# Down weights of the experts loaded with two neighbouring rows in each partition

## The reference

```
# for each expert e; h has 1024 columns, the expert's inner width is 3584
y   = (silu(h @ w_gate[e]) * (h @ w_up[e])) @ w_down[e]
out = out + combine[:, e] * y          # combine: weights of the top 2 of 8
```

## Time and profile before

| | us |
|---|---|
| median of three runs | 1332.88 |
| the three runs | 1332.56 to 1333.57 |
| the profiled execution | 1336.58 |
| its span, first to last instruction | 1335.0 |
| TensorE busy in it | 1305.1 (98%) |
| VectorE busy | 1134.6 (85%) |
| ScalarE busy | 936.9 (70%) |
| GpSimd busy | 149.3 (11%) |
| granted TensorE clock, mean | 0.998 of full speed |

### The profile page before, as it was taken

How to read it: one execution, slowest core, us unless ns; L and a number is a source line. 1 busy time by engine, 2 the same in 40 slices (tenths; PEclk the granted TensorE clock), 3 DMA queues, 4 the chain that set the end, 5 groups by cost and what they waited for, 6 DMA issues and landing times.

```text
span 1335.0 us, 17153 instructions
## 1 busy us (share of the span) xinstructions
PE 1305.1 (98%) x6789; PEld 1074.4 (80%) x6790; DVE 1134.6 (85%) x840; ACT 936.9 (70%) x800; POOL 149.3 (11%) x163
## 2 busy tenths in 40 slices
PE   9999999999999999999999999999999999999997
PEld 8879888898687678878887887788778878887886
DVE  6867666677678899999889999999999998989997
ACT  6675444465876777787777778777877787778774
POOL 3410000011042691000000000000000000000010
PEclk9999999999999999999999999999999999999999
DMA  9846555545369999999999999999999999999994
GB/s 319 247 156 199 190 190 189 189 157 188 121 227 289 395 394 394 395 387 394 363 387 394 393 366 395 395 392 372 394 395 384 358 388 395 392 360 384 396 395 189
DMA packets 199175, 430.81 MB, mean 323 GB/s; under 512 B 9784, under 2 KB 42832, under 8 KB 199088
## 3 DMA queue, kind: packets, MB, share of 16 engines
q1 hardware_dynamic: 193952, 415.40, 86.0%
q0 software_dynamic: 4592, 13.50, 2.7%
q10 hardware_dynamic: 544, 0.75, 0.2%
HBM read 417.56 MB, written 7.36 MB: 318 GB/s over the span
## 4 chain that ended last, share of the span: by engine, by line
PE 83%; DVE 8%; DMA 4%; ACT 2%; issue 2%; POOL 1%; SPq 0%; DVEq 0%; ACTq 0%; POOLq 0%
PE ps L1655 80%; DVE w_low L1156 6%; ACT w_high L808 2%; DMA raw<-in_moe_w_up 2%; PE ps L1982 1%; DMA raw<-in_w_in 1%; POOL work_b L615 1%; PE ps L1681 0%; PE ps L1817 0%; DMA hT_both<-hpad 0%; DMA work_b<-in_conv_w 0%; PE ps L1926 0%; DVE work_a L1530 0%; DVE act_both L1480 0%; DVE work_a L1513 0%
## 5 line engine op out<-in xcount | busy, mean ns | idle before, releaser
L1156 DVE TENSOR_TENSOR w_low<-raw,w_high 128x2048 fp32r<-128x2048 f32 x387 | 891.4, 2309 | 120.0 <-ACT w_high L808 117.9
L808 ACT ACTIVATE w_high<-raw 128x2048 fp32r<-128x2048 f32 x389 | 744.1, 1915 | 251.1 <-PE ps L1655 238.1
L1655 PE MATMUL ps<-w_high,hT_both 128*128 128x512 f32 (+1 forms) x1696 | 529.0, 389 | 3.2 <-DVE w_low L1156 3.1
L1655 PEld LDWEIGHTS ps<-w_high,hT_both 128*128 128x128 f32 x1696 | 316.6, 188 | 69.5 <-issue 3.8
L1655 PE MATMUL ps<-w_low,hT_both 128*128 128x512 f32 (+1 forms) x848 | 327.2, 386 | 0.0
L1655 PE MATMUL ps<-w_high,act_both 128*128 128x512 f32 x960 | 309.1, 393 | 5.7 <-DVE w_low L1156 5.7
L1655 PEld LDWEIGHTS ps<-w_high,act_both 128*128 128x128 f32 x960 | 180.8, 188 | 46.3 <-issue 9.3
L1655 PE MATMUL ps<-w_low,act_both 128*128 128x512 f32 x480 | 187.5, 391 | 0.0
L1655 PEld LDWEIGHTS ps<-w_low,hT_both 128*128 128x128 f32 x848 | 159.6, 188 | 30.4
L1655 PE MATMUL ps<-hT_both,w_high 128*128 128x256 f32 (+1 forms) x640 | 140.4, 339 | 0.0
L1655 PEld LDWEIGHTS ps<-hT_both,w_high 128*128 128x128 f32 x640 | 108.9, 190 | 11.2 <-DVE hT_both L1169 0.4
(11 more groups left out here) (317 smaller groups left out, 809.2 us busy)
## 6 DMA issues: line engine op xcount, KB each, us to landing
raw<-in_moe_w_gate SPq DMA_DIRECT2D x112, 1024.0 KB, 8.8
raw<-in_moe_w_up SPq DMA_DIRECT2D x112, 1024.0 KB, 8.8
raw<-in_moe_w_down SPq DMA_DIRECT2D x112, 1024.0 KB, 8.6
raw<-in_w_in SPq DMA_DIRECT2D x13, 1024.0 KB, 5.3
raw<-in_dense_w_gate SPq DMA_DIRECT2D x11, 1024.0 KB, 5.5
raw<-in_dense_w_up SPq DMA_DIRECT2D x11, 1024.0 KB, 5.5
raw<-in_dense_w_down SPq DMA_DIRECT2D x11, 1024.0 KB, 5.1
raw<-in_w_out SPq DMA_DIRECT2D x8, 1024.0 KB, 7.0
```

What stands on the lines that cost most here:

```text
L808: act.activation(w_part[0][:, s % PART_RING, :], raw[:, s % RAW_RING, :], ACT.Copy).then_inc(w_high_done, 1)
L1156: dve.tensor_tensor(w_part[1][:, q, :], raw[:, r, :], w_part[0][:, q, :], ALU.subtract).then_inc(w_low_done, 1)
L1655: return pe.matmul(out_, lhsT, rhs, start=start, stop=stop, skip_group_check=True)
```

## The change

The view of the experts' down weights now puts rows 2p and 2p + 1 of each 256 in partition p, in one run of 8 KB, in place of rows p and p + 128. Half f of the slot then holds the rows 2p + f. So that each row still meets its own column, the four turns of the product take, for load j and half f, the 128 columns 256 j + f, 256 j + f + 2, and so on: every second column, 8 bytes apart in `prod_t`. Number of loads, bytes, slots, matmuls and transposes stay as they are, and so do the copies after the turn and all of the dense layer.

```diff
         prod_t = work_a[:, 2560:3072]
+        prod_ff = prod_t.rearrange("t (j c f) -> t j c f", j=2, f=2)
...
-        ed_v = moe_w_down.rearrange("o e (k p) n -> (o e) p k n", p=P)
+        ed_v = moe_w_down.rearrange("o e (c p f) n -> (o e) p c (f n)", p=P, f=2)
...
             def down(s, e, g, i, per):
                 for j in range(2):
-                    load(s + j, ed_v[e, :, 4 * g + 2 * j:4 * g + 2 * j + 2, :], 2, i, per)
+                    load(s + j, ed_v[e, :, 2 * g + j:2 * g + j + 1, :], 1, i, per)
...
             def turn_small_act():
                 for f in range(4):
-                    last = pe.transpose(ps[:, 2, f * HALF:(f + 1) * HALF], prod_t[0:HALF, f * P:(f + 1) * P], ident[0:HALF, 0:HALF])
+                    last = pe.transpose(ps[:, 2, f * HALF:(f + 1) * HALF], prod_ff[0:HALF, f // 2, :, f % 2], ident[0:HALF, 0:HALF])
...
             def turn_act():
                 for f in range(4):
-                    last = pe.transpose(ps[:, 2, f * P:(f + 1) * P], prod_t[:, f * P:(f + 1) * P], ident[:, :])
+                    last = pe.transpose(ps[:, 2, f * P:(f + 1) * P], prod_ff[:, f // 2, :, f % 2], ident[:, :])
```

## The result

The changed kernel takes 1335.32 us, the median of 20 runs (1334.09 to 1337.28), against 1333.18 us for the kernel before (20 runs, 1331.35 to 1334.68). The ratio is 1.0017, with a 95% interval from 1.0010 to 1.0023. That is 2.1 us slower. It is under the 0.2% that I called the limit of a measurement, but with 20 runs on each side it stands clear of 1. I had forecast no change.

The account below looks back on a forecast made before the run. TensorE was taken to bound ordinary steps, with loads mattering only at the expert stage's start. Loads -0.3 us, turns 0 and the rest 0 took the median 1332.88 to 1332.6 us, range 1331.0 to 1336.5.

Parts of the forecast that it names:

- no change: Whole kernel: time stays within 1330.7 to 1335.5 us, given chance 0.81.
- What bounds the kernel: Expert stage: TensorE alone sets ordinary steps of 16.81 us; faster loads help only from about 412 to 462 us.
- The loads: Down loads at the expert stage's start: fewer packets save 0.05 us each, 0.3 us for six; bounds -0.5 to +1.2.
- The sign that I named for it: Expert stage start: ScalarE's waits for loads between 400 and 480 us fall from 12.6 us by some tenths.
- The turns: Transposes of the product on TensorE, 49 full and 7 small: strided reading costs 0, upper bound 24.3 us.
- Rival A: Transposes in the 56 turns: strided weight loads cost time, 1336 to 1357 us; chance 0.12.
- the sign that I gave for it: Transposes of the product: weight loads above 150 ns, or a turn above 0.49 us.
- Rival B: Down loads: 8 KB runs, or partitions 8 KB apart in memory, move slower; 1354 us at 3.2 us a load; chance 0.02.
- Rival C: Start of the expert stage: loads bind harder than thought, up to 4.31 us of TensorE idle returns, 1328.6 us; chance 0.05.
- Rival D: Down loads: descriptors are cut at 4 KB anyway, so loads stay unchanged, 1332.9 us; chance 0.15 of the 0.81.
- the sum: Whole kernel: loads -0.3 us, turns 0, the rest 0, giving 1332.6 us against the median.

Follow-up runs that it names:

- the loads alone: The changed kernel with its down loads in 8 KB runs but the transposes reading contiguous columns again: 1333.1 us, ratio 0.9999 to the kernel before.
- turns alone: The kernel before with transposes reading every second column and down loads still in 4 KB runs: 1337.3 us, ratio 1.0027.

## Why the prediction was wrong

**What bounds the kernel** stood. TensorE ends last in the ordinary steps, and the loads matter only at the start of the expert stage; no step there changed its length with the loads alone.

**The loads**: right in kind and within the bounds, a little low in size. I worked out 0.05 us a down load and 0.3 us in all, with a best case of 1.2, from a pair of loads that turned out to be no measure (2.62 us, where a down load takes 2.56). The landings give 0.06 to 0.07 us a load, 0.4 us for six. No run measures the total: the timed ratios of 0.9999 and twice 0.9995 agree with it and with no gain at all. The sign that I named for it didn't come: ScalarE's waits for loads between 400 and 480 us add up to 7.0 + 3.2 + 2.4 = 12.6 us in the changed kernel, the same as before, and to 11.7 in the second profile of the kernel before.

**The turns**: this is the step that failed, the sentence "I take no cost". The reason I gave, that 110 ns for 128 elements is a slow read with room for skipped bytes, took the spacing of the transposes for the pace of their weight loads. The loads need at most some 60 ns and wait for a matmul of 110. Read at a step they take about 120 ns, so there was no room for skipped bytes: the read runs at half its pace or less, and only the matmul beside it hid most of that. What was left: 0.03 us on a full turn and about 0.01 us more in the step behind it, and 0.17 us for a step with a small turn. The traces give 2.8 us for this term where I put 0, over all of the stage but its first four turns (3.3 with them, within the scatter of the start), and the timed turns alone 1.0027, 3.6 us.

The row that could have told me was in my own list: the small turn's weight loads had the same recorded 138 ns with matmuls of 64 columns. Their spacing of 0.06 us was one look away, and it bounds the pace of the load more tightly than the full turn does.

**Rival A** had the mechanism, the place and the direction, with a chance of 0.12, and the sign that I gave for it came: weight loads above 150 ns, at 201. Its price was mis-sized in the same way: I doubled the whole spacing (24.3 us) where only the excess of the load over the matmul counts (2.8 us). Had I bounded it so, with a load of at most 60 ns doubled to 120, the cost would have been 0 to 49 x 4 x 0.01 + 7 x 4 x 0.06 = 3.6 us, across the 2.7 us from which I call a kernel slower, and slower would have needed a chance near that of no change.

**Rival B**: no trace of it; a load with runs of 8 KB lands sooner. **Rival C**: fell; the loads alone gave no 4 us. **Rival D**: fell by the packet count.

**Numbers.** 1335.32 us lies in the range of 1331.0 to 1336.5, whose top I had left open for a partial cost of the turns, and even in the 1330.7 to 1335.5 that I called no change. The time lies there for the wrong reason, though: the sum had 0 for the turns, and I gave no change 0.81. Twenty runs on each side tell the 2.1 us from no change, where I had taken 2.7 as the limit. What I named as the sign of being wrong, an ordinary step of another length, is what happened: 16.85 in place of 16.81 us. One reading was also too smooth: the granted clock wasn't full throughout, as the earlier trace rows had it at 0.98, and the 3.4 us behind that are part of why the first profile stood 3.70 us above the median run.

## What to carry to other kernels

A weight load that hides behind a matmul shows its pace only where the matmul is short: look for the shortest one that uses the same kind of load before calling a load cheap, and price a slower load at what it has beyond the matmul, not at its full growth. When a layout change for DMA needs a permutation, look for an engine that can make it in a read it does anyway (here VectorE's read of its operands, PSUM among them, at every second column, at no cost in these runs), not in TensorE's stationary operand. And a gain in packets is worth what the stretch that waits for loads is worth, here under 0.1%.

## What the runs showed of the hardware that I had not expected

- A stationary float32 operand read at a step of two floats is recorded with 201 to 214 ns in place of 139, and a step of four costs the same (204 to 215 ns). Such loads follow each other in 120 ns, contiguous ones in some 60 or less. An fp32r load at a step of four is recorded with 309 ns in place of 188, and with a matmul of 512 columns beside it takes 236 ns in place of 227.
- A 1 MiB load behind others lands 2.71 us after the one before in packets of 2 KB, 2.56 in packets of 4 KB and 2.50 in packets of 8 KB: 8 to 9 ns for each packet of an engine.
- VectorE, 128x512 float32: 683 ns whether it reads every second float or all in order; 1104 ns when it walks in pairs and its write jumps.
- Two profiles of one kernel, 1336.58 and 1333.99 us, differ before 468 us alone: 0.9 us before the first turn of the stage and 1.9 in the four steps behind it, where the first has 3.4 us at the lower level of TensorE's clock. From there on they agree to a tenth of a microsecond over 850.
